# Shift and scale columns of an adaLN layer made in quarters of the k tiles instead of halves

## The chip, the core and the metric

The kernel runs on one core of a Trainium2 chip. The metric is the device time of one execution in microseconds. TensorE is called PE below, VectorE DVE, ScalarE ACT, GpSimd POOL, and SyncE SP; PEld is TensorE's weight load.

## What is computed

One decoder layer: a Mamba-2 branch and a sparse attention branch on one normalised and modulated input, merged by gates. Only the front of it is touched here:

```
def _layer(x, c, w_ada, b_ada, g_pre, ...):
    shift, scale, gate = jnp.split(c @ w_ada + b_ada, 3, axis=-1)
    h = _rmsnorm(x, g_pre) * (1.0 + scale[:, None, :]) + shift[:, None, :]
    z_ssm, xbc, dt_raw, q, kv, nsa_gate, z_att, merge_gate = jnp.split(h @ w_in, IN_SPLITS, axis=-1)
    ...
    return x + gate[:, None, :] * _rmsnorm(out, g_post)
```

x is 256 by 1024 and c is 1 by 1024, both float32; w_ada is 1024 by 3072. So h, 256 by 1024, needs one row of 2048 sums (shift and scale) over all 1024 rows of w_ada before its first column can exist, and every product of the layer needs h.

## The kernel before

Everything is held transposed: h has its 1024 columns on partitions, as 8 k tiles of 128, and 256 positions as the free size. A column tile of h @ w_in is 128 output columns; it sums 8 blocks, one for each k tile. Weights come as units of 128 by 1024 floats (512 KB), which is 8 blocks. Each unit goes through the same steps: SP loads it to one of 7 slots of `w_raw`; ACT rounds it to `w_hi` (`split_hi`, L927); DVE subtracts 6 of its 8 blocks to `w_lo` (`split_lo`, L1186) and POOL the rest (L1529); PE then does three matmuls for each block, hi by hi, hi by lo and lo by hi (L657 to L659 in the first ten units, L698 to L700 later). ACT and DVE are three units ahead of PE in casts and subtractions (`AHEAD`).

The start. `x_T` is squared on ACT (L1008), PE sums the squares over partitions with a matrix of ones (L570), ACT takes the root (L1011), DVE the reciprocal (L1295), and DVE scales x (L1299). Beside it PE multiplies `c` into `w_ada` (L579), with one column of weights at a time and four column groups of the array side by side, ACT copies the sums (`copy_rows`, L1017), PE turns them to columns (L588), DVE adds the bias (L1319) and makes the factor (L1323). Then ACT makes `h_hi` (L1023), DVE and POOL the full `h` (L1328, L1519), and DVE the rest `h_lo` (L1309), on which PE waits. All this happens in two halves of four k tiles: half 0 before the first weight matmul, half 1 at the step `ada2`.

The order of work. `weight_units` lists the units, `schedule` hangs the other steps after them. PE and POOL follow the list `STEPS`; ACT and DVE follow `LATE_STEPS`, in which the steps behind a unit come one unit later. Engines take their instructions strictly in their own order. The first ten units are five pairs of column tiles twice: units 0 to 4 hold k tiles 0 to 3 of ten column tiles, units 5 to 9 hold k tiles 4 to 7. All ten sums stay open in PSUM from unit 0 on. The tiles that end in units 5 to 9 are read out there: `dtg` (dt and gates) by ACT, `kc` and `vc` by two ACT copies each, and `b` 0 to 3 and `c` 0 by the convolution, which is one ACT pass (L960), three DVE taps (L1233), one ACT tanh (L969) and one DVE product (L1195). Units 10 to 12 are `c` 1 to 3, then four units of `x` and four of `z` alternate. `c` 1, `x` 0 and `x` 3 share the PSUM bank gemm0, `c` 2, `x` 1 and `z` 0 the bank gemm1, `c` 3, `x` 2 and `z` 1 the bank gemm2: PE may start the second of them only when DVE's taps on the first are done.

## Time and profile before

| | |
|---|---|
| median of 3 runs | 472.97 us (472.55 to 473.01) |
| the profiled execution | 471.68 us, of which the span 469.9 us |
| PE busy | 439.7 us, 94% of the span |
| DVE, ACT, POOL busy | 353.7, 258.8, 234.7 us |
| DMA | 84.04 MB, 179 GB/s over the span |

The span is what the trace shows; 1.8 us of the profiled execution lie around it. PE is busy almost throughout, so the time is PE's work plus the stretches in which it waits or runs at its lower clock. Most of these stretches lie in the first 90 us.

### The profile page before, as it was taken

How to read it: one execution, taken by the hardware profiler on the slowest of the kernel's cores; microseconds unless marked ns; L12 is line 12 of the kernel's file. 1: busy time of each engine (PE TensorE's matmuls, PEld its weight loads, DVE VectorE, ACT ScalarE, POOL GpSimd, SP SyncE). 2: the span in 40 equal slices, each digit the busy share in tenths (PEclk: the TensorE clock that was granted, in tenths of full speed). 3: DMA queues.
4: the chain of work that ended last, by engine and by line, in shares of the span. 5: the costliest groups of instructions: out<-in, count | busy, mean ns of one | idle time of the engine just before them, and what ended most of it. 6: DMA issues, size and time to landing. Idle time of an engine off the chain costs nothing.

```text
span 469.9 us, 9862 instructions
## 1 busy us (share of the span) xinstructions
PE 439.7 (94%) x3636; PEld 403.3 (86%) x3636; DVE 353.7 (75%) x617; ACT 258.8 (55%) x512; POOL 234.7 (50%) x236
## 2 busy tenths in 40 slices
PE   2689989999999999998799999999999999999995
PEld 2387989999999989886789999989898989999874
DVE  0466789999999999658898886678796767547733
ACT  3235885755564654466587845566465555534441
POOL 0155662368798689841374642245355362445440
PEclk9989999999999999999899999999999999999999
DMA  7999544564424544336419750725747443456102
GB/s 278 420 414 367 181 138 132 191 196 142 154 84 156 169 133 146 116 120 248 167 46 398 245 170 0 259 76 212 264 146 256 137 136 131 160 192 237 47 0 89
DMA packets 22391, 84.04 MB, mean 179 GB/s; under 512 B 2492, under 2 KB 2882, under 8 KB 21186
## 3 DMA queue, kind: packets, MB, share of 16 engines
q1 hardware_dynamic: 22344, 83.42, 50.4%
q8 instruction: 29, 0.48, 0.4%
q14 instruction: 18, 0.15, 0.1%
HBM read 82.36 MB, written 1.05 MB: 178 GB/s over the span
## 4 chain that ended last, share of the span: by engine, by line
PE 39%; DVE 8%; ACT 6%; issue 3%; DMA 1%; DVEq 0%; SPq 0%; ACTq 0%
PE gemm L698 8%; PE gemm L699 8%; PE gemm L700 8%; PE y_or_o L905 2%; ACT w_hi L927 2%; DVE w_lo L1186 2%; ACT probs L1144 1%; PE score L869 1%; DVE rstd_y L1406 1%; PE score L871 1%; DVE y_tmp L1411 1%; DVE ynorm_lo L1415 1%; DMA w_raw<-in_wpack 1%; PE small L623 1%; PE small L625 1%
## 5 line engine op out<-in xcount | busy, mean ns | idle before, releaser
L1529 POOL TENSOR_TENSOR w_lo<-w_raw,w_hi 128x256 fp32r<-128x256 f32 (+1 forms) x117 | 135.1, 1160 | 179.2 <-ACT w_hi L927 145.8
L698 PE MATMUL gemm<-h_hi,w_hi 128*128 128x256 f32 x600 | 174.0, 290 | 4.1 <-DVE w_lo L1186 1.9
L700 PE MATMUL gemm<-h_hi,w_lo 128*128 128x256 f32 x600 | 168.8, 281 | 0.0
L699 PE MATMUL gemm<-h_lo,w_hi 128*128 128x256 f32 x600 | 168.7, 281 | 0.0
L1186 DVE TENSOR_TENSOR w_lo<-w_raw,w_hi 128x768 fp32r<-128x768 f32 (+1 forms) x117 | 131.0, 1120 | 37.4 <-ACT w_hi L927 36.7
L927 ACT CAST w_hi<-w_raw 128x1024 fp32r<-128x1024 f32 x117 | 122.3, 1045 | 50.4 <-PE gemm L700 29.4
L698 PEld LDWEIGHTS gemm<-h_hi,w_hi 128*128 128x128 f32 x600 | 115.0, 192 | 7.1 <-issue 4.2
L699 PEld LDWEIGHTS gemm<-h_lo,w_hi 128*128 128x128 f32 x600 | 114.5, 191 | 1.0 <-issue 0.5
L700 PEld LDWEIGHTS gemm<-h_hi,w_lo 128*128 128x128 f32 x600 | 114.6, 191 | 0.0
L698 PE MATMUL gemm<-ynorm_hi,w_hi 128*128 128x256 f32 x128 | 36.4, 284 | 0.0
L700 PE MATMUL gemm<-ynorm_hi,w_lo 128*128 128x256 f32 x128 | 35.6, 278 | 0.0
L699 PE MATMUL gemm<-ynorm_lo,w_hi 128*128 128x256 f32 x128 | 35.6, 278 | 0.0
L1233 DVE SCALAR_TENSOR_TENSOR conv_acc<-gemm,conv_half,conv_acc 128x255 f32<-128x255 f32 (+2 forms) x66 | 31.6, 479 | 2.8 <-ACT conv_acc L960 1.2
L1144 ACT ACTIVATE probs<-score,softmax_small 128x128 f32<-128x128 f32 (+1 forms) x64 | 26.0, 421 | 1.3 <-DVE softmax_small L1450 1.3
L960 ACT ACTIVATE conv_acc<-gemm,conv_half 128x256 f32<-128x256 f32 x22 | 12.4, 563 | 24.4 <-DVE x_conv_T L1195 13.0
L698 PEld LDWEIGHTS gemm<-ynorm_hi,w_hi 128*128 128x128 f32 x128 | 24.1, 188 | 0.7 <-issue 0.7
L700 PEld LDWEIGHTS gemm<-ynorm_hi,w_lo 128*128 128x128 f32 x128 | 24.2, 189 | 0.0
L1541 POOL TENSOR_TENSOR seg_moving<-acs_rows,consts 128x512 fp32r<-128x512 f32 x16 | 20.0, 1269 | 8.2 <-DVE acs_cols L1375 8.2
L699 PEld LDWEIGHTS gemm<-ynorm_lo,w_hi 128*128 128x128 f32 x128 | 24.1, 188 | 0.0
L934 ACT ACTIVATE tanh_tmp<-gemm 128x256 f32<-128x256 f32 x24 | 9.2, 381 | 24.4 <-PE gemm L700 15.1
L1151 ACT COPY probs_T<-small 128x512 f32<-128x512 f32 x16 | 9.5, 593 | 19.8 <-PE y_or_o L905 19.8
L1462 DVE TENSOR_SCALAR probs<-probs,softmax_small 128x128 f32<-128x128 f32 (+1 forms) x64 | 18.8, 356 | 0.6
(252 smaller groups left out, 886.8 us busy)
## 6 DMA issues: line engine op xcount, KB each, us to landing
w_raw<-in_wpack SPq DMA_DIRECT2D x133, 512.0 KB, 4.3
w_ada_shift_scale<-in_w_ada SPq DMA_DIRECT2D x8, 1024.0 KB, 16.0
x_T<-in_xT SPq DMA_DIRECT2D x2, 512.0 KB, 6.1
x_residual<-in_x_tok SPq DMA_DIRECT2D x1, 1024.0 KB, 4.8
out_tok_dram<-out_tok SPq DMA_DIRECT2D x4, 256.0 KB, 2.1
ada_gate_products<-in_gate_bias SPq DMA_DIRECT2D x1, 512.0 KB, 4.8
g_post_rows<-in_g_post_rows SPq DMA_DIRECT2D x1, 512.0 KB, 5.0
consts<-in_consts SPq DMA_DIRECT2D x1, 272.0 KB, 22.1
```

Of the source, the lines that this page charges most:

```text
L698: nc.tensor.matmul(bank[:, 0:SEQ], w_hi, hi[:, k0 + k, :], start=first, stop=False)
L699: nc.tensor.matmul(bank[:, 0:SEQ], w_hi, lo[:, k0 + k, :], start=False, stop=False)
L700: last = nc.tensor.matmul(bank[:, 0:SEQ], w_lo, hi[:, k0 + k, :], start=False, stop=end)
L927: nc.scalar.copy(WH[:, n % HI_SLOTS, :], RAW[:, u % RAW_SLOTS, :]).then_inc(hi_ready, 1)
L960: nc.scalar.activation(ACC[:, ci % 2, :], bank, ACT.Identity, bias=CW[:, 96 + col:97 + col], scale=CW[:, 4 * col + 3:4 * col + 4]).then_in ...
L1144: last = nc.scalar.activation(E[:, k, b, P * qt:P * qt + nk], SB[qt][:, nk * b:nk * b + nk], ACT.Exp, bias=SM[:, k, 0, c:c + 1], accum_out ...
L1151: nc.scalar.copy(PT[:, i % 2, :, 0:SEQ], bank[:, :].rearrange("p (b q) -> p b q", b=2)).then_inc(release, 1)
L1186: nc.vector.tensor_tensor(WL[:, n % LO_SLOTS, 0:c], RAW[:, u % RAW_SLOTS, 0:c], WH[:, n % HI_SLOTS, 0:c], ALU.subtract).then_inc(lo_ready, 1)
L1233: ins = nc.vector.scalar_tensor_tensor(ACC[:, ci % 2, s:SEQ], bank[:, 0:SEQ - s], CW[:, 4 * col + tap:4 * col + tap + 1], ACC[:, ci % 2, s ...
L1462: nc.vector.tensor_scalar(e, e, SM[:, k, 3, 2 * qt + b:2 * qt + b + 1], None, ALU.mult).then_inc(p_done, 1)
L1529: nc.gpsimd.tensor_tensor(WL[:, n % LO_SLOTS, c:1024], RAW[:, u % RAW_SLOTS, c:1024], WH[:, n % HI_SLOTS, c:1024], ALU.subtract).then_inc( ...
L1541: nc.gpsimd.tensor_tensor(MV[:, c, :, :], TP[:, c, :].unsqueeze(1).to_broadcast([P, 4, P]), oh, ALU.mult).then_inc(mv_done, 1)
```

## The change

The shift and scale columns, and h with them, are made in four quarters of two k tiles. The first ten units hold the same 80 blocks in another order: for each quarter, two k tiles of ten column tiles, so that a quarter ends in the middle of a unit (20 blocks are two and a half units). The pieces of w_ada are half as large and their matmuls have 128 columns instead of 256, and twice as many. The matmuls for quarters 1 to 3 are spread among the weight matmuls, a piece before the blocks 4, 7, 9 and 11 of the quarter before, and the turn to columns before block 14. The squares of x are added over the k tiles on DVE, so that PE has one matmul with ones instead of eight. PE multiplies constants with constants where it would wait (`keep_busy`: 6, then 1 behind each of three pieces, then 3); the results are not used. All ten column tiles now end in units 7, 8 and 9. SP loads seven units before the last quarter of w_ada instead of five.

```
-    put(len(PAIRS) - 2, ("ada2", 0))
-    put(6, ("dtT", 0))
+    put(0, ("ada", 1))
+    put(2, ("ada", 2))
+    put(5, ("ada", 3))
+    put(8, ("dtT", 0))
...
+FIRST_BLOCKS = [(tile, QUARTER_K * q + k) for q in range(QUARTERS) for tile in FIRST_TILES for k in range(QUARTER_K)]
+FIRST_READ = {7: (("dtg", 0), ("b", 0)), 8: (("b", 1), ("kc", 0), ("kc", 1), ("b", 2)),
+              9: (("b", 3), ("vc", 0), ("vc", 1), ("c", 0))}
+ADA_PIECES_AT, ADA_COLUMNS_AT = (4, 7, 9, 11), 14
+KEEP_WARM = (6, 1, 3)
...
+            first_units = RAW_SLOTS
+            weights_before = {3: (0,), 4: (1, 2), 8: (3, 4), 12: (5, 6)}
+            for n in range(QUARTERS * HALF_K):
+                q, k = n // HALF_K, 2 * (n % HALF_K)
+                for u in weights_before.get(n, ()):
                     sp.dma_start(RAW[:, u, :], wpack[u]).then_inc(w_in[u], 16)
-                sp.dma_start(ADA[:, s, k:k + 2, :], w_ada1[:, s, k:k + 2, :]).then_inc(ada_in[n], 16)
+                sp.dma_start(ADA[:, q, k:k + 2, :], w_ada1[:, q, k:k + 2, :]).then_inc(ada_in[n], 16)
...
+            def keep_busy(n):
+
+                for _ in range(n):
+                    nc.tensor.matmul(GB[2][:, 0:256], cst("ones"), CS[:, 0:256], start=True, stop=True)
+
+            def ada_piece(q, piece):
+
+                pe.wait_ge(ada_in[HALF_K * q + piece], 16)
+                for k in range(2 * piece, 2 * piece + 2):
                     for j in range(4):
                         last = nc.tensor.matmul(ada_sums[32 * j:32 * j + 1, :], par("c", k, k + 1),
-                                                ADA[:, s, k, 256 * j:256 * j + 256], start=(k == 0), stop=(k == KT - 1))
-                last.then_inc(ada_full, 1)
+                                                ADA[:, q, k, P * j:P * j + P], start=(k == 0), stop=(k == KT - 1))
+                if piece == HALF_K - 1:
+                    last.then_inc(ada_full, 1)
...
+            keep_busy(KEEP_WARM[0])
+            for piece in range(HALF_K):
+                ada_piece(0, piece)
+                if piece == 1:
+                    pe.wait_ge(sq_summed, 1)
+                    nc.tensor.matmul(YB[:, 0:SEQ], cst("ones"), SQX[:, 0, :], start=True, stop=True).then_inc(ssx_full, 1)
+                if piece < HALF_K - 1:
+                    keep_busy(KEEP_WARM[1])
             ada_columns(0)
+            keep_busy(KEEP_WARM[2])
...
+                        if q + 1 < QUARTERS:
+                            if at in ADA_PIECES_AT:
+                                ada_piece(q + 1, ADA_PIECES_AT.index(at))
+                            if at == ADA_COLUMNS_AT:
+                                ada_columns(q + 1)
```

PE in the first units: before, all matmuls of the second half of w_ada stand in one block between unit 3 and unit 4 (L579, 32 instructions).

```order
L659 MATMUL score<-h_hi,w_lo 128x256
L579 MATMUL small<-w_ada_shift_scale,params 1x256 [waits ada_in4]
L579 MATMUL small<-w_ada_shift_scale,params 1x256 x7
L579 MATMUL small<-w_ada_shift_scale,params 1x256 [waits ada_in5]
L579 MATMUL small<-w_ada_shift_scale,params 1x256 x7
L579 MATMUL small<-w_ada_shift_scale,params 1x256 [waits ada_in6]
L579 MATMUL small<-w_ada_shift_scale,params 1x256 x7
L579 MATMUL small<-w_ada_shift_scale,params 1x256 [waits ada_in7]
L579 MATMUL small<-w_ada_shift_scale,params 1x256 x7
L657 MATMUL y_or_o<-h_hi,w_hi 128x256 [waits lo_ready,hi_ready]
```

Now each piece has eight instructions of 128 columns (L582) and stands between blocks of the gemm; this is the second piece of quarter 1, in unit 0.

```order
L671 MATMUL small<-h_hi,w_lo 128x256
L669 MATMUL gemm<-h_hi,w_hi 128x256 [waits lo_rest_ready]
L670 MATMUL gemm<-h_lo,w_hi 128x256
L671 MATMUL gemm<-h_hi,w_lo 128x256
L582 MATMUL small<-w_ada_shift_scale,params 1x128 [waits ada_in5]
L582 MATMUL small<-w_ada_shift_scale,params 1x128 x7
L669 MATMUL gemm<-h_hi,w_hi 128x256
```

There are twelve such pieces among the weight matmuls, where there was one block of four. ACT in the same stretch, of the changed kernel: the copy of the sums of quarter 1 (`ada_rows`, row 14) stands behind the casts of units 3 and 4, that of quarter 2 behind the casts of units 5 and 6.

```order
11 L937 CAST w_hi<-w_raw 128x1024 [waits w_in2]
12 L937 CAST w_hi<-w_raw 128x1024 [waits w_in3,cw_ready]
13 L937 CAST w_hi<-w_raw 128x1024 [waits unit_mm,w_in4]
14 L1027 COPY ada_rows<-small 128x128 [waits ada_full]
15 L1033 ACTIVATE h_hi<-x_T,mod,ada_scale 128x256 [waits ab]
16 L1033 ACTIVATE h_hi<-x_T,mod,ada_scale 128x256
17 L937 CAST w_hi<-w_raw 128x1024 [waits unit_mm,w_in5]
18 L937 CAST w_hi<-w_raw 128x1024 [waits unit_mm,w_in6]
19 L1027 COPY ada_rows<-small 128x128 [waits ada_full]
```

ACT where the ten tiles are read out. Before, the two table loads of the dt chain (L1070, L1072) stand between the casts of units 12 and 13, and `b` 2 is still the tile in hand.

```order
37 L927 CAST w_hi<-w_raw 128x1024 [waits unit_mm,w_in5]
38 L960 ACTIVATE conv_acc<-score,conv_half 128x256 [waits gated,unit_mm]
39 L969 ACTIVATE tanh_tmp<-conv_acc 128x256 [waits gated,free_gemm2_0]
40 L1070 ACT_TABLE_LOAD
41 L1070 ACTIVATE dt_work<-dt_work 128x64 [waits dt_u]
42 L1072 ACT_TABLE_LOAD
43 L1072 ACTIVATE dt_work<-dt_work 128x64 [waits dt_ln]
44 L927 CAST w_hi<-w_raw 128x1024 [waits unit_mm,w_in6]
```

Of the changed kernel, from the cast of unit 12 on: the readings of `b` 1, `kc` 0 and 1 and `b` 2 follow each other, and the two table loads (rows 54 and 56) now stand between the casts of units 14 (row 51) and 15 (row 58).

```order
51 L937 CAST w_hi<-w_raw 128x1024 [waits unit_mm,w_in0]
52 L970 ACTIVATE conv_acc<-gemm,conv_half 128x256 [waits gated,unit_mm]
53 L979 ACTIVATE tanh_tmp<-conv_acc 128x256 [waits gated,free_score1_0]
54 L1080 ACT_TABLE_LOAD
55 L1080 ACTIVATE dt_work<-dt_work 128x64 [waits dt_u]
56 L1082 ACT_TABLE_LOAD
57 L1082 ACTIVATE dt_work<-dt_work 128x64 [waits dt_ln]
58 L937 CAST w_hi<-w_raw 128x1024 [waits unit_mm,w_in1]
```

On DVE the taps of `b` 0 come first behind the subtraction for unit 11, where it was that for unit 9; from the taps of `c` 0 on the row of taps, products and subtractions is as before.

## Rows read from the trace of the kernel before

**Rows 1.** Waits of PE, 0 to 80 us: us in total, times, longest.
```profile
PE y_or_o L570 <- ACT x_sq L1008: 8.3, 1, 8.3
PE gemm L657 <- DVE h_lo L1309: 3.2, 2, 2.5
...
PE gemm L698 <- DVE conv_acc L1233: 1.3, 1, 1.3
```

**Rows 2.** Stretches: length, busy us (instructions) by engine, granted PE clock, DMA share, GB/s.
```profile
20.00:25.00 5.00, 1.94 (x19) 0.83 (x20) 2.60 (x8) 3.39 (x6) 1.63 (x3) 0.63 1.02 421
25.00:30.00 5.00, 5.00 (x32) 5.00 (x33) 4.41 (x7) 2.10 (x2) 2.41 (x2) 0.69 1.01 410
30.00:35.00 5.00, 5.00 (x46) 5.00 (x46) 1.86 (x2) 1.05 (x1) 2.72 (x2) 1.00 1.01 412
```

**Rows 3.** Timeline of the start: start us, us, engine, line, what [idle before].
```profile
8.31 6.72 PE L570 MATMUL y_or_o<-x_sq,consts 128*128 128x256 f32 x16 [8.31 <-ACT x_sq L1008]
...
15.64 1.75 DVE L1295 RECIPROCAL rstd_x<-rstd_x 128x256 f32<-128x256 f32 x1 [12.31 <-ACT rstd_x L1011]
17.43 1.23 DVE L1299 TENSOR_TENSOR x_T<-x_T,rstd_x 128x1024 f32<-128x1024 f32 x1
...
20.03 1.04 PE L579 MATMUL small<-w_ada_shift_scale,params 128*1 128x256 f32 x16 [2.30 <-DMA w_ada_shift_scale<-in_w_ada]
...
22.89 2.07 ACT L1023 ACTIVATE h_hi<-x_T,mod,ada_scale 128x256 fp32r<-128x256 f32 x4 [0.42 <-DVE ada_scale L1323]
...
24.80 0.55 PE L657 MATMUL gemm<-h_hi,w_hi 128*128 128x256 f32 x1 [2.54 <-DVE h_lo L1309]
```

**Rows 4.** Timeline of ACT: casts that wait for units 0, 5 and 6 to land.
```profile
17.51 1.04 ACT L927 CAST w_hi<-w_raw 128x1024 fp32r<-128x1024 f32 x1 [1.91 <-DMA w_raw<-in_wpack]
...
37.11 1.05 ACT L927 CAST w_hi<-w_raw 128x1024 fp32r<-128x1024 f32 x1 [3.41 <-DMA w_raw<-in_wpack]
38.39 1.05 ACT L927 CAST w_hi<-w_raw 128x1024 fp32r<-128x1024 f32 x1 [0.23 <-DMA w_raw<-in_wpack]
```

**Rows 5.** Timeline of PE around the second half of w_ada.
```profile
37.19 0.28 PE L659 MATMUL score<-h_hi,w_lo 128*128 128x256 f32 x1
...
38.26 2.77 PE L579 MATMUL small<-w_ada_shift_scale,params 128*1 128x256 f32 x48
40.96 0.39 PE L657 MATMUL y_or_o<-h_hi,w_hi 128*128 128x256 f32 x1
...
42.48 0.38 PE L588 MATMUL small<-consts,ada_rows 128*128 128x128 f32 x2
...
44.96 0.36 PE L657 MATMUL gemm<-h_hi,w_hi 128*128 128x256 f32 x1 [0.71 <-DVE h_lo L1309]
```

**Rows 6.** Timeline of PE: first matmul of unit 9, and of unit 13.
```profile
56.37 0.28 PE L657 MATMUL y_or_o<-h_hi,w_hi 128*128 128x256 f32 x1
...
68.74 0.39 PE L698 MATMUL gemm<-h_hi,w_hi 128*128 128x256 f32 x1 [1.33 <-DVE conv_acc L1233]
```

**Rows 7.** Timeline of ACT in the read-out of the ten tiles.
```profile
48.23 1.05 ACT L927 CAST w_hi<-w_raw 128x1024 fp32r<-128x1024 f32 x1 [1.72 <-PE gemm L659]
...
49.55 0.56 ACT L960 ACTIVATE conv_acc<-gemm,conv_half 128x256 f32<-128x256 f32 x1
...
52.48 1.28 ACT L969 ACT_TABLE_LOAD   x1
53.78 0.42 ACT L969 ACTIVATE tanh_tmp<-conv_acc 128x256 f32<-128x256 f32 x1
...
55.93 0.62 ACT L981 COPY kv_cmp_T<-small 128x256 f32<-128x256 f32 x2
```

**Rows 8.** Timeline of DVE: taps of `b` 0, subtraction for unit 13, taps of `c` 3.
```profile
50.19 1.51 DVE L1233 SCALAR_TENSOR_TENSOR conv_acc<-gemm,conv_half,conv_acc 128x255 f32<-128x255 f32 x3
...
63.13 1.09 DVE L1186 TENSOR_TENSOR w_lo<-w_raw,w_hi 128x896 fp32r<-128x896 f32 x1 [1.51 <-ACT w_hi L927]
...
72.97 1.51 DVE L1233 SCALAR_TENSOR_TENSOR conv_acc<-gemm,conv_half,conv_acc 128x255 f32<-128x255 f32 x3
```

More of the change, by code:

```diff
@@ L241 @@
 RAW_SLOTS, HI_SLOTS, LO_SLOTS = 7, 4, 4
-H_POOL = (2, 6)
-H_DVE = tuple(k for k in range(KT) if k not in H_POOL)
-EARLY_SPLITS = range(len(PAIRS), 17)
+EARLY_SPLITS = range(HALF_K + 1, 17)
 OUT_K = 2
@@ L564, in _ @@
             ident = cst("ident")
-            pe.wait_ge(cst_in_s, 16)
-            for k in range(KT):
-                if k % HALF_K == 0:
-                    pe.wait_ge(sqx_done, k // HALF_K + 1)
-                last = nc.tensor.matmul(YB[:, 0:SEQ], cst("ones"), SQX[:, k, :], start=(k == 0), stop=(k == KT - 1))
-            last.then_inc(ssx_full, 1)
-            def ada_rows(s):
-                for k in range(KT):
-                    if k % 2 == 0:
-                        pe.wait_ge(ada_in[HALF_K * s + k // 2], 16)
+            def keep_busy(n):
+                for _ in range(n):
+                    nc.tensor.matmul(GB[2][:, 0:256], cst("ones"), CS[:, 0:256], start=True, stop=True)
@@ L637, in weight_unit @@
                     return
[L638 removed]
+                if kind == "first":
                     n = SPLIT_IDX[u]
@@ L660, in weight_unit @@
+                        w_lo = WL[:, n % LO_SLOTS, P * c:P * c + P]
+                        first = k == 0 and tile not in SECOND_HALVES
+                        end = k == KT - 1 and tile not in FIRST_HALVES
+                        nc.tensor.matmul(bank, w_hi, HH[:, k, :], start=first, stop=False)
+                        nc.tensor.matmul(bank, w_hi, HL[:, k, :], start=False, stop=False)
+                        last = nc.tensor.matmul(bank, w_lo, HH[:, k, :], start=False, stop=end)
                     last.then_inc(unit_mm, 1)
@@ L1338, in _ @@
             scale_x(1)
-            for n in range(2, AHEAD):
-                split_lo(n)
+            split_lo(2)
+            for q in range(2, QUARTERS):
+                scale_x(q)
             done = ()
@@ L1709, in lay_out @@
             wpack[u] = ada[:, part, 2048:3072]
-        elif kind == "pair":
-            both = [tiles[k][n].reshape(P, KT, P)[:, HALF_K * part:HALF_K * (part + 1)] for k, n in PAIRS[j]]
-            wpack[u] = np.stack(both, 2).reshape(P, 1024)
+        elif kind == "first":
+            blocks = [tiles[tile[0]][tile[1]].reshape(P, KT, P)[:, k] for tile, k in FIRST_BLOCKS[8 * j:8 * j + 8]]
+            wpack[u] = np.concatenate(blocks, 1)
         elif kind == "out":
```

173 lines of the change are left out of this document (76 added, 97 removed).

## The prediction

> **What bounds the kernel now.** I read the busy shares first: PE works 94% of the span, so only PE's waits, its slow stretches and its added work count. Then PE's waits: the large ones of the first 80 us are 8.3 us for the squares, 3.2 us for h_lo and 1.3 us for the convolution taps [rows 1]. The stretches show the rest. The granted clock is 0.63 and 0.69 from 20 to 30 us; with PE busy all through, 32 matmuls ran in 25 to 30 us against 46 in the next five [rows 2], so the slow clock costs 14 matmuls of 0.11 us, 1.5 us. DMA moves 410 to 421 GB/s there, its share is full [rows 2]: the start is bound by the transfer of w_ada. The timeline says how: the last piece of half 0 is multiplied at 20.03, ACT makes h_hi at 22.89, and PE's first weight matmul is at 24.80 [rows 3]. The second view that matters is later: unit 13 (`x` 0) starts at 68.74, released by DVE's taps on `c` 1 after 1.33 us of idling [rows 6]. From 63.13 on DVE stands in a queue of its own: its last wait is 1.51 us for a cast [rows 8]. Whatever comes early to this place must get through that queue.
>
> **Landings, the clock of the start.** Transfers land in the order of issue. Units 5 and 6, of 512 KB, land 1.28 us apart [rows 4], 0.41 MB in a microsecond, and unit 0 lands at 17.5, behind x and three 1 MB pieces [rows 4]. With 1.26 us for 512 KB, x is there at 8.8 (17.5 less one unit and three pieces) and the new order lands thus: pieces of quarter 0 at 10.1, 11.3, 12.6 and 15.1, units 0, 1, 2 at 13.8, 16.3, 17.6, quarter 1 at 18.9 to 22.6, units 3 and 4 at 23.9 and 25.2, quarter 2 at 26.4 to 30.2, units 5 and 6 at 31.5 and 32.7, quarter 3 at 34.0 to 37.7, unit 7 at 39.7. The transfers are half as large. The Trainium skill, "DMA: Bandwidth & Descriptors", section "Bandwidth", asks for 1 MiB or more in one DMA and would speak against that; the units show 512 KB at the full rate when many are under way, so by the trace this costs nothing.
>
> **First weight matmul.** The chain from the last piece's matmul to PE's first was 4.8 us (20.03 to 24.80) [rows 3]. From 15.1 it would be 19.9. It has half of the matmuls and one column turn and one bias operation less, about 0.9 us. So 19.0, 5.8 us earlier. The x chain stays hidden: squares done at 9.9, five additions on DVE done at about 11.5 (half and quarter of the 1.23 us row), one matmul instead of 6.7 us of them, root, 1.75 us reciprocal, half of 1.23 us scaling [rows 3], subtraction of unit 0: 16.4, against 16.5 for the columns. That cover is thin: all that makes it later goes through.
>
> **Price of the pieces.** In the stream, 64 matmul records of 256 columns took from 37.19 to 40.96, less one ordinary step of 0.11: 3.66 us [rows 5]. 48 of them start within 2.77 less a tail of 0.38 us, 0.051 apart; four column groups run side by side, so a group takes 0.21 and sixteen 3.4 us, and 0.3 us is switching. A new piece is 16 records of 128 columns. Half the columns is 0.44 us; with all or half of the switching, 0.6 to 0.8. Bounds: 0.44 (no switching), and 1.15 (no cheaper with half the columns: 16 by 0.051, and 0.34). I take 0.68, since the groups' spacing is that of their columns. Twelve pieces are 8.2 us where 3.7 stood: 4.5 us more PE work. Three single turns instead of two pairs' worth add about 0.3 us.
>
> **The ledger of the ten first tiles.** A block is 0.34 us, a unit 2.72. Quarter 0: from 19.0, 14 blocks (4.8) and four pieces (2.7) reach the columns of quarter 1 at 26.5. Their rows are copied on ACT behind the cast of unit 4, which lands at 25.2 and is cast until 26.3: 26.55. So PE hardly waits, but cannot gain here either: were it earlier, it would wait for that cast. From columns to the next quarter's first matmul it was 2.48 us (42.48 to 44.96) [rows 5]; with two operations fewer ahead I take 2.0, plus 0.35 in which DVE still has unit 4's subtraction: quarter 1 starts at 28.9. PE's other six blocks last as long, so the wait of 0.71 [rows 5] and the gaps around it, 1.4 together, go. Quarters 1 and 2 take 20 blocks, four pieces and a turn, 9.7 us each, with their rows, casts and landings ahead in time: quarter 3 starts at 48.3. Four blocks end unit 7 at 49.7, and unit 8 ends at 52.4. Before, unit 9 started at 56.37 [rows 6]. That is 4.0 us ahead: 5.8 for the start, 1.5 for the clock, 1.4 for waits gone, less 4.8 for pieces and turns.
>
> **The queue behind it.** This gain meets the read-out. Before, the ten tiles ended in units 5 to 9, now in units 7 to 9, in 5.4 us less. Count from t, the end of unit 8. ACT's cast started 3.27 us after the first matmul of the unit it waited for (44.96 to 48.23) [rows 5, 7], and that unit took 3.0 with its stalls, so some 0.26 behind a unit's end: cast 12 ends 1.3; `conv_acc` of `b` 1 (0.56) 1.8; table load (1.28) 3.1; tanh of `b` 0 (0.42) 3.5 [rows 7]. DVE's taps on `b` 1 run from 2.2 to 3.7 (1.51) [rows 8]; ACT's tanh of `b` 1 follows to 4.2, two copies (0.62) 4.7, `conv_acc` of `b` 2 5.2. DVE: taps `b` 2 to 6.7, subtraction 13 (cast ends 6.7) to 7.7, taps `b` 3 to 9.2; ACT's tanh of `b` 3 9.7, copies, `conv_acc` of `c` 0 10.7; DVE: taps `c` 0 12.2, subtraction 14 (1.0) 13.2, taps `c` 1 14.7. So unit 13 starts at t + 14.7, where PE could at t + 11.2: a wait of 3.5 us where 1.33 stood, at 67.1. Then two table loads stand before cast 15, which ends at 16.8; before, they were done long ahead. DVE subtracts 15 to 17.85, taps `c` 2 to 19.3 (a second wait of PE, some 2 us), product, subtraction 16, and begins the taps on `c` 3 at t + 20.6. Before they began at 72.97 [rows 8], 16.6 after unit 8's end. The queue eats 4.0 us, and 52.4 + 20.6 = 73.0.
>
> **Sum.** 5.8 + 1.5 + 1.4 − 4.8 − 4.0 = about 0. From the taps on `c` 3 the orders are the same and DVE leads until unit 17, then PE: the difference stays. The profiled execution of before took 471.68 us around its span of 469.9, the median is 472.97, 1.3 above it; a change of zero gives 473.0 for the median. Less or more than 0.2% (0.95 us) is about what a measurement can tell from no change.
>
> **Rivals.**
> - Faster: the queue costs less. From the taps of `b` 0 to those of `c` 1 DVE has six sets of taps (1.51), three subtractions (1.0) and four products (0.4): 13.6 us of work [rows 8], which would end at t + 13.1 instead of 14.7, and casts with nothing to wait for would bring `c` 3 to t + 18.3. Then 2.3 us are gained; with pieces at 0.58 another 0.8 in quarters 1 and 2. 470.7 with one, 469.9 with both, 472 with half of one. For it: ACT waits by its order only. Against: each wait of the ledger follows from that order. Chance 0.34 for this side.
> - Slower: PE comes to the first weight matmul at the lower clock. Before, it fell to 0.63 after only the pieces and a pause [rows 2, 3], and the new start is single pieces and single constant products with pauses of one microsecond. Then 14 matmuls' worth, 1.5 us, is lost again, quarter 1's columns slip from 26.5 to 28, and nothing later absorbs it: 474.5. The place is 17 to 22 us, and it decides if the row there shows under 0.95. Chance 0.23.
> - Slower: pieces bound by the number of instructions, 1.15 us each. Quarter 1's columns then wait for PE until 28.4, and quarters 1 and 2 take 1.9 us longer each: 5.6 us, 478.6. Against it: 0.051 us fits the columns exactly. Chance 0.07. The Trainium skill, "TensorE: Matmul & The Clock Gate", section "Wait — 56ns, not 53.3ns?", names some 62 ns for each matmul where the sequencer handles it in software; by that, an estimate, a piece would be 1.0 us and the sum near 477. The trace has 0.051 us from record to record, below that figure.
> - The change does nothing at the front, since x and not w_ada is late: the first matmul then comes at up to 20.2 instead of 19.0, 474.2. It is part of the slower side.
>
> **How the numbers follow.** Forecast "no difference" 0.36, with its own range 472.0 to 473.9; faster side 0.34; slower side 0.30. The range goes from 470.7 (the queue as DVE's work alone) to 475.6 (lower clock, and pieces at 0.8).
>
> **What would show it.** Right: first weight matmul near 19.0 at a granted clock of 1; pieces of 8 instructions costing 0.6 to 0.8; unit 8 ending near 52.4; unit 13 waiting 3 to 4 us for DVE's taps, unit 14 again about 2. Wrong: unit 13 starting before 65 (the queue is shorter) or after 70; a granted clock near 0.5 at 19 to 22 us; waits of PE for `ada_rows` or h_lo over 1 us at a quarter's start. In particular, the ledger fails if ACT's casts of units 3 and 4 come later than 26.3, since the copy of rows stands behind them.

## The result and the profile after

The changed kernel takes 476.14 us (median of 12 runs, 474.92 to 478.71) against 472.99 (12 runs of before on the same chip): ratio 1.0063, 95% interval 1.0046 to 1.0081. It is 3 us slower, and the range of the forecast, 470.7 to 475.6, does not hold the median. The profiled execution took 474.92 us around a span of 473.1, where before had 471.68 and 469.9.

The start came out close to the forecast. Timeline of PE in the changed kernel (start us, us, engine, line, what [idle before]); it answers to [rows 3]:

```profile
3.44 5.10 PE L575 MATMUL gemm<-consts 128*128 128x256 f32 x12 [3.44 <-DMA consts<-in_consts]
10.12 0.62 PE L582 MATMUL small<-w_ada_shift_scale,params 128*1 128x128 f32 x16 [1.58 <-DMA w_ada_shift_scale<-in_w_ada]
...
11.91 0.70 PE L600 MATMUL y_or_o<-x_sq,consts 128*128 128x256 f32 x2
...
15.21 0.62 PE L582 MATMUL small<-w_ada_shift_scale,params 128*1 128x128 f32 x16 [0.99 <-DMA w_ada_shift_scale<-in_w_ada]
16.22 0.33 PE L590 MATMUL small<-consts,ada_rows 128*128 128x128 f32 x1 [0.39 <-ACT ada_rows L1027]
...
18.63 0.36 PE L669 MATMUL gemm<-h_hi,w_hi 128*128 128x256 f32 x1 [0.78 <-DVE h_lo L1326]
```

The first weight matmul is at 18.63 (19.0 forecast, 24.80 before). The granted clock is 1 there, where [rows 2] had 0.63 and 0.69. What is lost begins behind it. The next stretches of the same view are the last piece of quarter 1 and its columns, the first and the second block of quarter 1, the same two of quarter 2, the first matmul of quarter 3, and the end of unit 8 (the matmul behind it belongs to the dt chain):

```profile
25.12 0.28 PE L671 MATMUL gemm<-h_hi,w_lo 128*128 128x256 f32 x1
25.33 0.62 PE L582 MATMUL small<-w_ada_shift_scale,params 128*1 128x128 f32 x16
25.88 0.39 PE L669 MATMUL gemm<-h_hi,w_hi 128*128 128x256 f32 x1
26.10 0.28 PE L670 MATMUL gemm<-h_lo,w_hi 128*128 128x256 f32 x1
...
27.04 0.27 PE L590 MATMUL small<-consts,ada_rows 128*128 128x128 f32 x1
...
29.27 0.28 PE L669 MATMUL gemm<-h_hi,w_hi 128*128 128x256 f32 x1
...
30.02 0.39 PE L669 MATMUL gemm<-h_hi,w_hi 128*128 128x256 f32 x1 [0.24 <-DVE h_lo L1326]
...
39.83 0.28 PE L669 MATMUL gemm<-h_hi,w_hi 128*128 128x256 f32 x1
...
40.35 0.39 PE L669 MATMUL gemm<-h_hi,w_hi 128*128 128x256 f32 x1
...
50.18 0.28 PE L669 MATMUL gemm<-h_hi,w_hi 128*128 128x256 f32 x1
...
54.26 0.38 PE L724 MATMUL small<-consts,dt_gate_T 128*128 128x128 f32 x2
```

From 25.12 to 25.88 are 0.76 us where two matmuls of the gemm stand 0.12 apart, and the matmul behind the piece also holds PE 0.22 instead of 0.12: a piece costs 0.75. Quarters 1, 2 and 3 start at 29.27, 39.83 and 50.18; the forecast had 28.9, 38.6 and 48.3. The matmuls at 30.02 and 40.35 are the second blocks of quarters 1 and 2: each k tile has its own `h_lo`, and the second is not ready when PE comes to it (0.75 us from the first block to the second in quarter 1, 0.52 in quarter 2, where a block takes 0.35). Unit 8 ends at 54.25 instead of 52.4.

Then the read-out queue. Timeline of DVE, which answers to [rows 8], from the taps of `c` 0 to those of `c` 3:

```profile
65.40 1.51 DVE L1243 SCALAR_TENSOR_TENSOR conv_acc<-score,conv_half,conv_acc 128x255 f32<-128x255 f32 x3 [0.58 <-ACT conv_acc L970]
66.83 1.21 DVE L1196 TENSOR_TENSOR w_lo<-w_raw,w_hi 128x896 fp32r<-128x896 f32 x1
67.97 1.50 DVE L1243 SCALAR_TENSOR_TENSOR conv_acc<-gemm,conv_half,conv_acc 128x255 f32<-128x255 f32 x3
...
71.47 1.25 DVE L1196 TENSOR_TENSOR w_lo<-w_raw,w_hi 128x896 fp32r<-128x896 f32 x1 [1.67 <-ACT w_hi L937]
72.64 1.50 DVE L1243 SCALAR_TENSOR_TENSOR conv_acc<-gemm,conv_half,conv_acc 128x255 f32<-128x255 f32 x3
...
74.47 1.34 DVE L1196 TENSOR_TENSOR w_lo<-w_raw,w_hi 128x896 fp32r<-128x896 f32 x1
75.73 1.50 DVE L1243 SCALAR_TENSOR_TENSOR conv_acc<-gemm,conv_half,conv_acc 128x255 f32<-128x255 f32 x3
```

The taps on `c` 3 begin 2.76 us later than the 72.97 of [rows 8]. Timeline of PE there, unit 13's first matmuls and one behind the low clock:

```profile
69.53 0.58 PE L710 MATMUL gemm<-h_hi,w_hi 128*128 128x256 f32 x1 [3.97 <-DVE conv_acc L1243]
69.90 0.41 PE L711 MATMUL gemm<-h_lo,w_hi 128*128 128x256 f32 x1
70.12 0.41 PE L712 MATMUL gemm<-h_hi,w_lo 128*128 128x256 f32 x1
...
73.00 0.28 PE L711 MATMUL gemm<-h_lo,w_hi 128*128 128x256 f32 x1
```

PE idles 3.97 us before unit 13 (1.33 in [rows 6]) and comes back at the lower clock: the matmuls are 0.21 apart until 72.9, then 0.12. The stretches (length, busy us with instructions of PE, PEld, DVE, ACT, POOL, granted PE clock, DMA share, GB/s) say the same:

```profile
70.00:71.00 1.00, 1.00 (x7) 1.00 (x7) 0.00 (x0) 0.99 (x3) 0.32 (x1) 0.50 0.74 291
...
73.00:74.00 1.00, 1.00 (x11) 1.00 (x9) 0.93 (x3) 0.14 (x1) 1.00 (x2) 1.00 0.00 0
```

### The profile page after: what moved, and what is told of

Same layout as the page of the kernel before. It is cut to its first block, busy times and chain, and to the rows that moved or that the text cites. A ratio compares the mean times of both kernels' runs of the same rounds, so it can differ in the third digit from the quotient of the medians.

```text
span 473.1 us, 10156 instructions
## 1 busy us (share of the span) xinstructions
PE 446.3 (94%) x3774; PEld 407.3 (86%) x3774; DVE 358.0 (76%) x624; ACT 259.6 (55%) x514; POOL 232.9 (49%) x238
## 4 chain that ended last, share of the span: by engine, by line
PE 44%; DVE 6%; ACT 4%; issue 3%; DVEq 0%; ACTq 0%
PE gemm L710 10%; PE gemm L712 10%; PE gemm L711 10%; PE y_or_o L915 2%; ACT w_hi L937 1%; ACT probs L1154 1%; PE score L879 1%; DVE rstd_y L1416 1%; PE score L881 1%; DVE w_lo L1196 1%; PE small L633 1%; PE small L635 1%; PE score L635 1%; PE small L634 1%; PE score L634 1%
## 5 line engine op out<-in xcount | busy, mean ns | idle before, releaser
L1538 POOL TENSOR_TENSOR w_lo<-w_raw,w_hi 128x256 fp32r<-128x256 f32 (+1 forms) x117 | 131.8, 1132 | 172.2 <-ACT w_hi L937 139.0
L712 PE MATMUL gemm<-ynorm_hi,w_lo 128*128 128x256 f32 x128 | 35.6, 278 | 0.0
L711 PE MATMUL gemm<-ynorm_lo,w_hi 128*128 128x256 f32 x128 | 35.6, 278 | 0.0
L944 ACT ACTIVATE tanh_tmp<-gemm 128x256 f32<-128x256 f32 x24 | 9.2, 382 | 24.4 <-PE gemm L712 15.2
## 6 DMA issues: line engine op xcount, KB each, us to landing
w_ada_shift_scale<-in_w_ada SPq DMA_DIRECT2D x16, 512.0 KB, 14.5
```

Of the source, the lines that this page charges most:

```text
L711: nc.tensor.matmul(bank[:, 0:SEQ], w_hi, lo[:, k0 + k, :], start=False, stop=False)
L712: last = nc.tensor.matmul(bank[:, 0:SEQ], w_lo, hi[:, k0 + k, :], start=False, stop=end)
L1538: nc.gpsimd.tensor_tensor(WL[:, n % LO_SLOTS, c:1024], RAW[:, u % RAW_SLOTS, c:1024], WH[:, n % HI_SLOTS, c:1024], ALU.subtract).then_inc( ...
```

## The experiments

Each run stands against the kernel before on its own chip. Diffs are against the changed kernel unless they say otherwise. Ratios are with 95% intervals; 0.001 is 0.47 us. "Slower than the changed kernel" is the difference of two such ratios, so it is less certain than either: where the two intervals overlap, the time alone does not show it.

**1. `second_half_pairs`: quarters at the front, the second half in the order of before.**

```
-FIRST_BLOCKS = [(tile, QUARTER_K * q + k) for q in range(QUARTERS) for tile in FIRST_TILES for k in range(QUARTER_K)]
+FIRST_BLOCKS = [(tile, QUARTER_K * q + k) for q in range(2) for tile in FIRST_TILES for k in range(QUARTER_K)]
+FIRST_BLOCKS += [(tile, HALF_K + k) for i in range(0, 10, 2) for k in range(HALF_K) for tile in FIRST_TILES[i:i + 2]]
...
+for _q, _blocks in ((1, (4, 7, 9, 11, 14)), (2, (20, 21, 22, 24, 27)), (3, (30, 31, 32, 33, 36))):
...
-    put(5, ("ada", 3))
-    put(8, ("dtT", 0))
+    put(3, ("ada", 3))
+    put(6, ("dtT", 0))
```

> Quarters 0 and 1 as changed, but the blocks of k tiles 4 to 7 stand in the order of before: units 5 to 9, one pair of tiles each, so the ten tiles end in units 5 to 9 again. The pieces of quarters 2 and 3 both stand among the blocks of quarter 1, the dt chain hangs on units 6 to 10 again. Theory 'read-out queue': the loss of the change is the queue of ten tiles that end in three units. Quarter 1 starts at 30.0 as in the changed kernel; 20 blocks of 0.355, eight pieces of 0.75 and two turns reach unit 5 at 43.4, where before had 44.96; unit 13 waits about 1.3 us as before, no slow clock there, the taps of c 3 begin at about 71.3 (72.97 before, 75.73 changed), and the profiled execution takes 470.0, ratio to before 0.9965. Rival 'PE work': the loss comes from pieces, turns and switches among the weight matmuls; all of them are still here, so the time stays within 0.1% of the changed kernel's (ratio 1.006).

Measured: 0.9970 (0.9953 to 0.9988). All pieces, turns and switches are still there, and the kernel is now faster than before. So the placing of the tiles' ends decides the sign, not the pieces. (With the tiles' ends the dt chain goes back to its old units, and the pieces of quarters 2 and 3 stand at other blocks.) The expectation starts from quarter 1 at 30.0; in the changed kernel that is its second block.

**2. `before_late_ends`: that part of the change alone, in the kernel before.** The ten tiles end in units 7 to 9, and the dt chain, which needs one of them, hangs on units 8 to 11 as in the change. Against the kernel before:

```
+SECOND_BLOCKS = [(tile, HALF_K + 2 * q + k) for q in range(2) for pair in PAIRS for tile in pair for k in range(2)]
...
-PAIR_READ = (PAIRS[0], (("b", 1),), (("kc", 0), ("kc", 1), ("b", 2)), (("b", 3),), (("vc", 0), ("vc", 1), ("c", 0)))
+PAIR_READ = ((), (), PAIRS[0], (("b", 1), ("kc", 0), ("kc", 1), ("b", 2)), (("b", 3), ("vc", 0), ("vc", 1), ("c", 0)))
```

> The kernel before with one edit: the blocks of k tiles 4 to 7 in the order of the changed kernel (k tiles 4 and 5 of all ten tiles, then 6 and 7), so that the ten tiles end in units 7, 8 and 9; the dt chain hangs on units 8 to 11 as in the change. Start, pieces, squares and clock are those of before. Theory 'read-out queue': unit 8 ends at 56.4 as before, the taps on c 3 begin 21.5 us later instead of 16.6, at 77.9 where 72.97 stood; 4.9 us slower, ratio 1.0100 to 1.0105. Unit 13 waits about 6 us with a low clock behind it. Rival 'queue hidden' (ACT and DVE have room, my forecast of the queue as DVE's work alone): at most 2.5 us slower, ratio 1.005 or less.

Measured: 1.0096 (1.0072 to 1.0119), 4.5 us slower. Timeline of PE, unit 5, the last matmul of unit 8 and unit 13:

```profile
45.94 0.36 PE L663 MATMUL gemm<-h_hi,w_hi 128*128 128x256 f32 x1 [0.69 <-DVE h_lo L1315]
...
56.84 0.28 PE L665 MATMUL gemm<-h_hi,w_lo 128*128 128x256 f32 x1
...
71.93 0.39 PE L704 MATMUL gemm<-h_hi,w_hi 128*128 128x256 f32 x1 [3.70 <-DVE conv_acc L1239]
```

and of DVE, the taps on `c` 3:

```profile
78.12 1.50 DVE L1239 SCALAR_TENSOR_TENSOR conv_acc<-gemm,conv_half,conv_acc 128x255 f32<-128x255 f32 x3
```

Unit 8 ends at 56.95, one matmul (0.11) behind its last one, and the taps on `c` 3 begin 21.2 us behind that, where before had 16.6 ([rows 6, 8]). In this trace the queue costs 4.6 us by itself, and the measured 4.5 agree. The wait at unit 13 is 3.7 and not the 6 that I expected, for unit 13 can only be late by the taps on `c` 1; the rest falls on the units behind it, where the granted clock is 0.84 from 70 to 75 us and 0.82 from 75 to 80.

**3. `pieces_together`: the four pieces of a quarter stand before block 11.**

```
-                            if at in ADA_PIECES_AT:
-                                ada_piece(q + 1, ADA_PIECES_AT.index(at))
+                            if at == ADA_PIECES_AT[-1]:
+                                for piece in range(HALF_K):
+                                    ada_piece(q + 1, piece)
```

> The changed kernel, but the four pieces of a quarter stand together before block 11 of the quarter before, instead of before blocks 4, 7, 9 and 11. Theory 'switching': a piece is 0.44 us of columns and 0.3 us of changing from weight matmuls to it and back; nine changes go, quarters 1 and 2 take 0.9 us less each and quarter 0 0.4, unit 8 ends 2.2 us earlier and the time falls by 2.2 us (ratio to before 1.0015). Rival 'instructions': a piece costs its 16 instructions wherever it stands, 0.74 us; the time stays (ratio 1.006). Rival 'waits': with the pieces later the rows come later, PE waits at the starts of quarters 2 and 3, and the time rises.

Measured: 1.0016 (0.9997 to 1.0035), 2.2 us less than the changed kernel for nine switches fewer; the two intervals do not overlap. Timeline of PE around the first block of pieces:

```profile
24.22 0.28 PE L672 MATMUL gemm<-h_hi,w_lo 128*128 128x256 f32 x1
24.43 1.93 PE L582 MATMUL small<-w_ada_shift_scale,params 128*1 128x128 f32 x64
26.29 0.39 PE L670 MATMUL gemm<-h_hi,w_hi 128*128 128x256 f32 x1
```

64 records in 1.93 us, less a tail of 0.27, are 0.026 apart, half of the 0.051 of 256 columns ([rows 5]): 0.42 us for a piece. The block holds the gemm for 2.07 us from start to start, less an ordinary step of 0.12 and with the 0.10 that the matmul behind it is longer: 2.05, where four single pieces cost 3.0. So the change from weight matmuls to a piece and back costs 0.32 us, and nine of them are 2.8 us, of which 2.2 reach the end.

**4. `busy_in_wait` and `busy_in_wait_8`: does the low clock behind the wait cost anything?** Ahead of unit 13, 34 and 8 products of constants:

```
+                if (kind, j) == ("x", 0):
+                    for tile in (("vc", 0), ("vc", 1)):
+                        wait_tile_out(pe, tile)
+                    for _ in range(8):
+                        nc.tensor.matmul(YB[:, 0:256], cst("ones"), CS[:, 0:256], start=True, stop=True)
```

> The changed kernel, and PE multiplies constants 34 times (0.11 us each) in front of unit 13, in the 3.97 us in which it waits for the taps on c 1; the products go to a bank that is free. Theory 'queue': the clock stays at 1 behind the wait, unit 13 takes 2.8 us instead of 4.4, but PE then stands at unit 14 until the taps on c 2 are done (74.15) and at unit 15 until those on c 3 are; the time falls by 0.4 us at most, ratio to before 1.0055 to 1.0065. Rival 'clock': the 1.5 us that the low clock costs at 69.5 to 72.7 are on the path; the time falls by 1.5 us, ratio 1.003.

Measured: 1.0219 (1.0195 to 1.0243). My price of a constant product was wrong, and the run answers nothing on the clock. Timeline of PE:

```profile
65.81 14.84 PE L679 MATMUL y_or_o<-consts 128*128 128x256 f32 x68
80.29 0.47 PE L715 MATMUL gemm<-h_hi,w_hi 128*128 128x256 f32 x1
```

The constants are multiplied unrounded: two records, 0.216 us apart, for each product, 0.43 us, where the rounded operands of the weight matmuls need one record and 0.12. The 34 products hold PE until unit 13 starts at 80.29, 10.8 us later than in the changed kernel. (The next expectation has 0.40 us and an end at 79.4, from a stretch that ended at 79 us, in the middle of the products.) With 8 of them:

> The changed kernel with 8 constant products in the wait before unit 13. The run with 34 of them showed that one takes 0.40 us (13.5 us from 65.81 to 79.4), so 8 take 3.2 us and end before the taps on c 1. Theory 'queue': the clock stays at 1, but PE waits at unit 14 for the taps on c 2; the time falls by 0.4 us at most, ratio to before 1.0055 to 1.0065. Rival 'clock': the low clock of 69.5 to 72.7 is on the path, the time falls by 1.5 us, ratio 1.003.

Measured: 1.0069 (1.0052 to 1.0085), no faster than the changed kernel. Timeline of PE, and the stretch behind it:

```profile
66.24 3.62 PE L679 MATMUL y_or_o<-consts 128*128 128x256 f32 x16
70.38 0.39 PE L715 MATMUL gemm<-h_hi,w_hi 128*128 128x256 f32 x1 [0.53 <-DVE conv_acc L1248]
74.77 0.71 PE L740 MATMUL small<-consts,adt 128*128 128x128 f32 x4 [1.38 <-POOL adt L1595]
```

```profile
70.00:74.00 4.00, 3.00 (x24) 2.80 (x24) 2.31 (x4) 3.99 (x6) 2.17 (x5) 1.00 0.33 123
```

The clock stays at 1 and unit 13 takes its normal time, but PE then idles 1.38 us for POOL ahead of `acs`. The taps on `c` 3 begin 7.77 us behind those on `c` 1, in the changed kernel 7.76, and from unit 9 to unit 17 PE needs 31.51 us, there 31.47. The low clock filled a wait that would have been there anyway.

**5. `no_constants` and `before_constants`: the clock at the start.** The first is the changed kernel with `KEEP_WARM = (0, 0, 0)`. The second is the kernel before with constant products in its waits:

```
             pe.wait_ge(cst_in_s, 16)
+            keep_busy(6)
             for k in range(KT):
...
+                        if s == 0 and k:
+                            keep_busy(3)
                         pe.wait_ge(ada_in[HALF_K * s + k // 2], 16)
...
             ada_columns(0)
+            keep_busy(3)
```

> The changed kernel without the constant products at the start. Theory 'clock at the start': PE comes to its first weight matmul at the lower clock, the granted clock at 18 to 22 is 0.5 to 0.7, matmuls of the gemm start 0.21 apart instead of 0.12 for about 3 us, and quarter 1 starts 1.5 us later; nothing absorbs it, ratio to before 1.0095. Rival 'pieces suffice': the single pieces hold the clock as they are, the time is that of the changed kernel, ratio 1.006.

> The kernel before, with nothing added but constant products in its waits at the start: 6 ahead of the squares, 3 ahead of each later piece of half 0, 3 behind the columns. Theory 'clock': PE comes to its first weight matmul at clock 1, the 14 matmuls' worth lost at 24.8 to 28 come back, and all later work with them: 1.5 us faster, ratio 0.9965 to 0.997. Rival: half 1 of w_ada sets the start of unit 5 anyway, so an earlier unit 4 only waits longer; the time stays within 0.1%.

Measured for `no_constants`: 1.0092 (1.0068 to 1.0117), 1.4 us slower than the changed kernel, with intervals that overlap. Measured for `before_constants`: 0.9968 (0.9951 to 0.9985), 1.5 us faster than before. Stretches of `no_constants`:

```profile
15.00:20.00 5.00, 1.72 (x20) 1.16 (x20) 4.57 (x9) 3.44 (x6) 2.31 (x3) 0.69 1.03 414
20.00:25.00 5.00, 5.00 (x48) 4.07 (x50) 4.21 (x5) 0.76 (x2) 1.28 (x1) 0.63 1.02 406
```

The clock is 0.69 and 0.63 where the changed kernel has 1.00. PE was idle 2.59 us before its first weight matmul here. From the first weight matmul to unit 9 this trace needs 1.4 us more than that of the changed kernel (37.14 for 35.77), so the trace says the same as the time. Timeline of PE in `before_constants`, the first weight matmul and unit 5:

```profile
24.48 0.36 PE L666 MATMUL gemm<-h_hi,w_hi 128*128 128x256 f32 x1 [1.24 <-DVE h_lo L1318]
...
43.94 0.36 PE L666 MATMUL gemm<-h_hi,w_hi 128*128 128x256 f32 x1 [1.06 <-DVE h_lo L1318]
```

From the first weight matmul to unit 4 it is 1.53 us shorter than before, to unit 5 only 0.70 (19.46 for 20.16), and PE waits 1.06 us there instead of 0.71. So the rival, that half 1 sets the start of unit 5, holds for half of the gain in this trace; the median gained 1.5 us all the same. The constants are worth about 1.5 us in the kernel before, and probably as much in the changed one.

**6. `ones_on_pe`: the squares.** Eight products with ones instead of one, no additions on DVE:

```
-                    pe.wait_ge(sq_summed, 1)
-                    nc.tensor.matmul(YB[:, 0:SEQ], cst("ones"), SQX[:, 0, :], start=True, stop=True).then_inc(ssx_full, 1)
+                    for k in range(KT):
+                        pe.wait_ge(sqx_done, k // HALF_K + 1)
+                        last = nc.tensor.matmul(YB[:, 0:SEQ], cst("ones"), SQX[:, k, :], start=(k == 0), stop=(k == KT - 1))
+                    last.then_inc(ssx_full, 1)
```

> The changed kernel with the squares summed by eight products with ones on PE again, in the place of the one product, and no additions on DVE. Theory 'x chain': eight products of 0.40 us run from 11.9 to 15.1 instead of one, so root and reciprocal come 2.8 us later, and since the x chain was as long as the chain through w_ada, the first weight matmul comes about 2 us later, at 20.5 to 21; ratio 1.010 to 1.011. Rival 'hidden': PE has that time free at the start, the transfer of w_ada sets the end, ratio 1.006.

Measured: 1.0093 (1.0063 to 1.0123), by that ratio 1.4 us slower than the changed kernel, but the intervals overlap, and by the medians (479.70 us, before 474.00) it is more. Timeline of PE, the eight products and the first weight matmul:

```profile
12.55 4.49 PE L601 MATMUL y_or_o<-x_sq,consts 128*128 128x256 f32 x16
...
22.63 0.36 PE L671 MATMUL gemm<-h_hi,w_hi 128*128 128x256 f32 x1 [1.42 <-DVE h_lo L1321]
```

The first weight matmul comes 4.0 us later than in the changed kernel and not 2. The granted clock was 0.57 from 10.5 to 14.5 us, under the products, and 0.57 again from 24 to 28 us, in spite of the constants; so this trace holds a loss of clock beside that of the products. The six executions fall in two groups, 477.3 and 477.4 us with a mean granted clock of 0.992 and 0.993, the others 479.5 to 480.9 us with 0.982 to 0.985. How much the products cost alone stays open. That the x chain is as long as the chain through w_ada can be read from the trace of the changed kernel: the columns are made at 16.22 to 16.55, and DVE, which must scale x and subtract unit 0 first, comes to the bias at 17.03. So the x chain is even the longer one, by 0.5 us.

**7. `dt_later`: the two table loads moved out of the queue.** `dtB` and `dtL` hang on unit 12 instead of 10, `dtC` on 13, `acs` on 15.

> The changed kernel with the second part of the dt chain (two table loads of 1.28 us on ACT, before cast 15) hung on unit 12 instead of 10, its last step on 13 and the acs step on 15. Theory 'loads in the queue': DVE's wait of 1.67 us for cast 15 goes, the taps on c 3 begin at 74.1 instead of 75.7, unit 13 starts as before at 69.5; the two loads come back where ACT waits for DVE (waits of 0.9 to 1.5 us behind each conv_acc of the x tiles in the earlier runs), so part is kept: the time falls by 0.7 to 1.6 us, ratio 1.003 to 1.005. Rival 'queue by DVE's work': the time stays, ratio 1.006.

Measured: 1.0166 (1.0147 to 1.0185), 4.9 us slower than the changed kernel. DVE's wait for cast 15 went (the taps on `c` 3 begin 5.56 us behind those on `c` 1, instead of 7.76), but it came back larger two units on, and a second one took its place on PE. Timeline of DVE and of PE:

```profile
78.29 1.24 DVE L1196 TENSOR_TENSOR w_lo<-w_raw,w_hi 128x896 fp32r<-128x896 f32 x1 [2.27 <-ACT w_hi L937]
```

```profile
89.38 0.91 PE L746 MATMUL small<-c_T,b_T 128*128 128x128 f32 x5 [3.58 <-DVE eps_columns L1386]
```

The loads (74.20 and 75.77 on ACT) now hold cast 17. And `acs`, two units later, keeps the small bank which `cb` needs: PE stands 3.58 us. The run shows that ACT has no free place for the loads so soon behind; it can't say what they cost where they are.

**8. `exp_for_ln`: the loads taken away where they stand.** The kernel leaves out the logarithm, so its dt is not that of the layer.

```
-                    nc.scalar.activation(DTW[:, 4], DTW[:, 3], ACT.Ln).then_inc(dt_ln, 1)
+                    nc.scalar.activation(DTW[:, 4], DTW[:, 3], ACT.Exp).then_inc(dt_ln, 1)
```

> The changed kernel with an exponential in the place of the logarithm of the dt chain, so that ACT needs no table loads between the casts 14 and 15; dt is computed wrongly for that, everything else stands in the same order. Theory 'order of ACT': of the 4.9 us that the read-out queue costs, DVE's wait of 1.67 us for cast 15 comes from the two loads (2 x 1.28 us): unit 13 starts at 69.5 as before, the taps on c 3 1.5 to 1.7 us earlier, and the time falls by as much less what the low clock of PE takes (PE reaches unit 14 at 74.6 whatever DVE does, so of the 1.6 us about 0.4 is left at unit 14 and the rest at unit 17): ratio to before 1.003 to 1.0055. Rival 'work of DVE': the loads are hidden, ratio 1.006.

Measured: 1.0049 (1.0028 to 1.0069). Timeline of DVE, the taps on `c` 1 and `c` 3:

```profile
69.62 1.50 DVE L1243 SCALAR_TENSOR_TENSOR conv_acc<-gemm,conv_half,conv_acc 128x255 f32<-128x255 f32 x3
...
75.61 1.50 DVE L1243 SCALAR_TENSOR_TENSOR conv_acc<-gemm,conv_half,conv_acc 128x255 f32<-128x255 f32 x3
```

They are 5.99 apart instead of 7.76, so in the trace the loads cost 1.77 us of the queue. From unit 9 to unit 17 PE needs 29.99 us instead of 31.47, so 1.5 of them reach unit 17. Of the whole time only 0.7 us is seen, and the intervals of this ratio and of the changed kernel's overlap; how much of the 1.77 reaches the end stays open.

**9. `quarters_then_half` and `columns_38`: what the runs point to.** Order of blocks as in 1, pieces together, rows of quarter 1 ahead of the casts of units 3 and 4, quarter 3 loaded ahead of units 5 and 6:

```
+for _q, _first, _columns in ((1, 9, 11), (2, 25, 27), (3, 33, 35)):
+    ADA_AT[_first] = [("piece", _q, _piece) for _piece in range(4)]
+    ADA_AT[_columns] = [("columns", _q)]
...
-            weights_before = {3: (0,), 4: (1, 2), 8: (3, 4), 12: (5, 6)}
+            weights_before = {3: (0,), 4: (1, 2), 8: (3, 4)}
...
             act.wait_ge(cw_ready, 1)
+            copy_rows(1)
+            make_h_hi(1)
```

> A version made of what the runs showed: quarters 0 and 1, then k tiles 4 to 7 in the pair order of before; the four pieces of a quarter together (before blocks 9, 25 and 33, columns before 11, 27 and 35); the rows of quarter 1 copied ahead of the casts of units 3 and 4; SP loads quarter 3 ahead of units 5 and 6; dt chain as before. Theory: quarter 1 starts at 28.5 to 29.3, unit 5 at 40.0 to 41.0 (44.96 before), and the queue stands to unit 5 as before (taps on c 3 28.0 to 28.5 behind it, at 68.5 to 69.5), so 4 us faster: profiled 467.5 to 468.5, ratio 0.991 to 0.993. Rival 'transfer': quarter 3 and unit 5 land too late when PE is this early; then ratio 0.996 or more, with waits of PE for w_ada or h_lo over 1 us between 30 and 42.

Measured: 0.9913 (0.9896 to 0.9930), 469.37 us, 4.1 faster than before. Timeline of PE, the columns of quarter 3, unit 5 and unit 13:

```profile
38.53 0.30 PE L595 MATMUL small<-consts,ada_rows 128*128 128x128 f32 x1 [1.03 <-ACT ada_rows L1030]
...
40.38 0.28 PE L672 MATMUL gemm<-h_hi,w_hi 128*128 128x256 f32 x1
...
64.81 0.39 PE L713 MATMUL gemm<-h_hi,w_hi 128*128 128x256 f32 x1 [1.45 <-DVE conv_acc L1248]
```

Unit 5 starts 4.6 us earlier than the 44.96 of [rows 5], unit 13 3.9 earlier than in [rows 6], with nearly the same wait. Several things were changed at once here, and the runs do not say what each is worth. The 1.03 us at 38.53 was aimed at next, with `(3, 33, 38)` in place of `(3, 33, 35)`:

> The version of quarters and a half with one number changed: the turn to the columns of quarter 3 stands before block 38 instead of 35. There PE waited 1.03 us for the copied rows, which stand on ACT behind the cast of unit 5 (37.17, its landing). Theory: with three blocks in that wait the columns come at the same time, 38.5, the wait goes, unit 5 starts at 39.4 instead of 40.4 and h of k tiles 6 and 7 is still in time (40.8); ratio to before 0.989 to 0.990. Rival 'queue': DVE's read-out has no room left, the gain turns into a longer wait at unit 13 (2.4 us instead of 1.45), ratio 0.991 as without it.

Measured: 0.9901 (0.9878 to 0.9925). The wait for the rows went, but a new one of 0.46 us, for POOL's share of unit 5, stands at 43.48 in its trace. The two versions can't be told apart by their intervals.

**10. `z_early` and `z_early_2`: a unit without taps ahead of `c` 1.** Against `columns_38`:

```
-    units += [("c", j, 0) for j in range(1, 4)]
+    units += [("z", 0, 0)] + [("c", j, 0) for j in range(1, 4)]
```

> As columns_38, and the tile z 0 (one tanh and one product, no taps) is unit 10, ahead of c 1 to 3 and x, instead of unit 17. Theory 'queue': DVE has a convolution tile in each unit of 2.84 us from unit 5 on (taps 1.51, product 0.42, subtraction 1.0: 2.9 us); one unit without taps gives it 2.5 us back, the wait of PE at the unit after c 3 (1.4 us) and the one of 0.5 at unit 17 go, ratio 0.986 to 0.987. Rival: the wait only moves, since ACT's casts hold the taps; ratio 0.989 to 0.991.

Measured: 1.0044 (1.0027 to 1.0062). Timeline of PE:

```profile
79.75 2.05 PE L749 MATMUL small<-c_T,b_T 128*128 128x128 f32 x8 [5.16 <-DVE c_T L1210]
```

The step `cb` kept its unit number while `c` 3 moved back by one, and PE stood before it 5.16 us. With `acs` on 14 and `cb` on 16 to 18:

> z 0 as unit 10 as in the run before, with the steps behind it moved by the unit that c 3 and x moved: acs on unit 14 instead of 13, cb on 16 to 18 instead of 15 to 17. In the run before, PE stood 5.16 us in front of cb, which waits for the product of c 3. Theory 'DVE's work': with that wait gone the unit without taps gives DVE 2.5 us back; PE's wait at unit 13 stays (1.6 us, now for the product of z 0), the one of 0.5 at unit 17 goes; ratio to before 0.987 to 0.989. Rival: the wait comes back at x 0 to x 2; ratio 0.990 or more, as columns_38.

Measured: 0.9914 (0.9891 to 0.9938). The 5.16 are gone, unit 13 waits 0.95 us, unit 17 no more, and still the time is that of `columns_38` within the intervals: one light unit for DVE gives nothing that can be measured. PE waits 1.0 us less in the trace; where that went was not followed.

## Why the prediction was wrong

The forecast was "no difference", 473.0; it came out 3 us slower. The mechanisms held: an earlier start, pieces that cost PE, and a read-out queue that takes the gain back. What failed is the size of two terms of the sum, "4.8 for pieces and turns" in the ledger of the ten first tiles and "4.0" for the queue, and both erred on the same side.

- **First weight matmul, clock.** Right: 18.63 for 19.0, clock 1. The closeness is in part luck, since kernels with the same start had it at 17.99 to 19.92 us. The x chain was not hidden, as the prediction had it by 0.1 us, but 0.5 us the longer one (run 6). Run 5 shows the 1.5 us of the constants for the kernel before, and for the changed one its trace agrees. The rival of a cold PE did not come; it would have, without them.
- **Price of the pieces, ledger of the ten tiles.** The step that failed first. From the first weight matmul to the end of unit 8 I had 33.4 us (19.0 to 52.4), and it took 35.6 (18.63 to 54.25). Three terms were too small. A piece costs 0.75 and not 0.68: of columns 0.42, as taken, but of switching 0.32 (run 3) where I had taken 0.24; that is 0.8 us over twelve. A block takes 0.35 us in most of this stretch and not 0.34, since the matmuls are 0.118 us apart and not 0.113: about 0.5 us over the three quarters. And the second block of quarters 0, 1 and 2 waits for its own `h_lo`, 0.43, 0.40 and 0.17 us longer than a block; the ledger put that at nothing, as it took a quarter's h to be ready at once. Quarters 0, 1 and 2 took 10.64, 10.56 and 10.35 us where 9.9, 9.7 and 9.7 were forecast. With the 0.4 us that the start came earlier, unit 8 ends 1.85 late. Of the 4.0 us that were to be ahead at this point, 2.1 were.
- **The queue.** Right in its mechanism, and shown alone by run 2: 4.5 us there. In the changed kernel, counted again from t, the end of unit 8, the taps on `c` 1 end at t + 15.2 (14.7 forecast) and those on `c` 3 begin at t + 21.5 (20.6): 4.9 instead of 4.0. Of these 0.9 us some 0.6 are three subtractions that I had at 1.0 us each, 14 to 16, and that hold DVE 1.14, 1.17 and 1.26 us to the next taps; the rest was not followed. The forecast wait of 3.5 us before unit 13 was 3.97; DVE's waits of 0.58 twice and of 1.67 for cast 15 are those of the ledger. The second wait of PE, 2 us at unit 14, did not show: PE lost that time at the lower clock instead, and run 4 shows that it cost nothing more. I had not thought of the clock falling behind my own wait of 3.5 us, although it falls in the kernel before too, between 21 and 22 us, behind a pause of 2.30 us and the last piece (20.03 in [rows 3]). The queue of run 2 holds the place of the dt chain's two table loads as well: taken away, they give back 1.77 us of it in the trace (run 8). So the late ends of the tiles and the loads that move with them are one cost of 4.9 us here, and the loads are at most 1.8 of it.
- **Sum.** 1.85 and 0.9 are the 2.76 us by which the taps on `c` 3 are late. At unit 17 it is still 2.75 (85.87 for 83.12), at the end of the span 3.2; the last 0.4 was not followed.
- **The rivals.** "The queue costs less" had 0.34 and is refuted: its 13.6 us of DVE work would need casts that wait for nothing, and the waits that follow from ACT's order were all there. "Bound by the number of instructions" is refuted as well: with half the columns the records are 0.026 apart and not 0.051 (run 3). The Trainium skill, "TensorE: Matmul & The Clock Gate", section "Wait — 56ns, not 53.3ns?", has 62 ns for each matmul where the sequencer handles it in software. Here an instruction is two records, so instructions are 0.053 us apart, and that bound does not show. The Trainium skill, "DMA: Bandwidth & Descriptors", section "Bandwidth", advises transfers of 1 MiB or more. Smaller ones cost nothing here: the stretches from 15 to 35 us move 405 to 413 GB/s with pieces of 512 KB.

Split by runs: quarters at the front and constants are worth 1.4 us (run 1), or 4.1 with the pieces together, the rows early and quarter 3 loaded early (run 9); the tiles that end in three units, with the dt chain behind them, cost 4.5 (run 2). The change is the first with the second, 3.1 us by this sum and 3.0 measured.
